# Order of VectorE's work behind a norm: the rest of a chunk behind the first product of the next pair

## The reference, cut to what matters

```python
def _rms_norm(x, w):
    xf = x.astype(jnp.float32)
    y = xf * lax.rsqrt(jnp.mean(xf * xf, axis=-1, keepdims=True) + RMS_EPS)
    return (y * w.astype(jnp.float32)).astype(x.dtype)
...
x = x + _rms_norm(mix, W['norm_mix_post'][i])
h = _rms_norm(x, W['norm_ffn_pre'][i])
...                                   # f = a dense SwiGLU in layer 0, a top-2-of-8 mixture in layer 1
x = x + _rms_norm(f, W['norm_ffn_post'][i])
gate = jax.nn.sigmoid(_rms_norm(x, W['norm_ple'][i]) @ W['ple_w_gate'][i])
x = x + gate * (p[i].astype(x.dtype) @ W['ple_w_proj'][i])
```

## Time and profile before

| | us |
|---|---|
| median of 3 runs | 1734.22 (1734.21 to 1734.29) |
| the profiled execution | 1737.75 |
| its span, first to last instruction | 1736.0 |
| PE busy in the span | 1674.9 (96%) |
| VectorE busy | 690.6 (40%) |
| ScalarE busy | 568.2 (33%) |
| GpSimd busy | 254.1 (15%) |
| mean granted clock of TensorE | 0.98 |

### The profile page before, as it was taken

How to read it: one execution, slowest core, us unless ns; L and a number is a source line. 1 busy time by engine, 2 the same in 40 slices (tenths; PEclk the granted TensorE clock), 3 DMA queues, 4 the chain that set the end, 5 groups by cost and what they waited for, 6 DMA issues and landing times.

```text
span 1736.0 us, 29438 instructions
## 1 busy us (share of the span) xinstructions
PE 1674.9 (96%) x12422; PEld 1542.4 (89%) x12422; DVE 690.6 (40%) x1039; ACT 568.2 (33%) x955; POOL 254.1 (15%) x323
## 2 busy tenths in 40 slices
PE   7999998999999998989999979999999999999988
PEld 6877898999999997988778968998988989889988
DVE  3444355444244434554444552314133142242355
ACT  5232444322122323442324452313233132231252
POOL 5643121000000001206421012000000000002010
PEclk9999999999999999999999986999999999999999
DMA  5345261323232321313352325787877877879312
GB/s 171 87 87 114 75 208 60 92 90 113 71 97 85 115 80 49 127 56 80 89 114 73 103 104 195 234 284 243 276 281 227 290 258 245 295 233 340 114 50 86
DMA packets 73062, 260.02 MB, mean 150 GB/s; under 512 B 10152, under 2 KB 10672, under 8 KB 72928
## 3 DMA queue, kind: packets, MB, share of 16 engines
q1 hardware_dynamic: 59760, 219.52, 38.9%
q0 software_dynamic: 13184, 38.79, 8.0%
HBM read 237.20 MB, written 21.31 MB: 149 GB/s over the span
## 4 chain that ended last, share of the span: by engine, by line
PE 92%; DVE 3%; ACT 2%; issue 1%; DMA 1%; ACTq 0%; DVEq 0%; SPq 0%; POOL 0%; POOLq 0%
PE lin L728 72%; PE aux L728 18%; DVE h_lo L1784 1%; DVE zreg L1781 1%; DMA region_y<-yslot,idxg 1%; ACT h_hi L1266 1%; PE aux L1031 1%; DVE zreg L1784 0%; DVE x L1781 0%; PE aux L1033 0%; DMA wreg<-in_w_in_slabs 0%; ACT region_y L1266 0%; PE aux L873 0%; PE aux L875 0%; ACT zreg L1297 0%
## 5 line engine op out<-in xcount | busy, mean ns | idle before, releaser
L728 PE MATMUL lin<-h_hi,whi 128*128 128x260 f32 x1616 | 434.1, 289 | 23.2 <-DVE h_lo L1784 23.2
L728 PE MATMUL lin<-h_lo,whi 128*128 128x260 f32 x1616 | 425.9, 285 | 0.0
L728 PEld LDWEIGHTS lin<-h_hi,whi 128*128 128x128 f32 x1616 | 309.3, 191 | 32.9 <-issue 27.3
L728 PE MATMUL lin<-h_hi,wlo 128*128 128x260 f32 x1616 | 329.1, 286 | 0.0
L728 PEld LDWEIGHTS lin<-h_lo,whi 128*128 128x128 f32 x1616 | 309.0, 191 | 0.6
L728 PE MATMUL lin<-zreg,wreg 128*128 128x160 f32 x2048 | 284.2, 301 | 1.7 <-issue 1.7
L728 PEld LDWEIGHTS lin<-zreg,wreg 128*128 128x128 f32 x2048 | 280.6, 191 | 4.8 <-issue 4.7
L728 PEld LDWEIGHTS lin<-h_hi,wlo 128*128 128x128 f32 x1616 | 252.8, 191 | 0.0
L1781 DVE TENSOR_TENSOR wlo<-wreg,whi 128x1024 fp32r<-128x1024 f32 (+1 forms) x140 | 180.5, 1290 | 90.1 <-ACT whi L1266 90.1
L1266 ACT ACTIVATE whi<-wreg 128x1024 fp32r<-128x1024 f32 (+1 forms) x140 | 152.0, 1089 | 68.2 <-DMA wreg<-in_ffn_w_down 26.9
L1781 DVE TENSOR_TENSOR region_b<-zreg,lin 128x160 f32<-128x160 f32 x88 | 28.2, 321 | 320.8 <-PE lin L728 320.8
(11 more groups left out here) (341 smaller groups left out, 2454.8 us busy)
## 6 DMA issues: line engine op xcount, KB each, us to landing
wreg<-in_moe_w_gate SPq DMA_DIRECT2D x64, 512.0 KB, 5.2
wreg<-in_moe_w_up SPq DMA_DIRECT2D x64, 512.0 KB, 6.0
wreg<-in_moe_w_down SPq DMA_DIRECT2D x56, 512.0 KB, 4.5
wreg<-in_w_in_slabs SPq DMA_DIRECT2D x44, 512.0 KB, 3.6
ring_more<-in_moe_w_gate SPq DMA_DIRECT2D x24, 512.0 KB, 4.6
ring_more<-in_moe_w_up SPq DMA_DIRECT2D x24, 512.0 KB, 4.5
wreg<-in_ffn_w_gate SPq DMA_DIRECT2D x22, 512.0 KB, 3.5
wreg<-in_ffn_w_up SPq DMA_DIRECT2D x22, 512.0 KB, 3.4
```

The lines of the kernel that those rows point to most:

```text
L728: return nc.tensor.matmul(out, lhsT, rhs, start=start, stop=stop)
```

## The change

```diff
             def normed(N, w, h=None, sums=None):
 
-                for c in range(DC + 2):
-                    if h is not None and c >= 2:
+                def product(c):
+                    if N or c >= 2:
+                        dve.wait_ge((x_dve, x_pool)[c % 2], N * DC // 2 + c // 2)
+                    stt(ut[:, c % 2], acc[:, c], cols[:, w + c:w + c + 1], rn, ALU.mult, ALU.mult).then_inc(ut_ready, 1)
+                for c in range(0, DC + 2, 2):
+                    if c < DC:
+                        product(c)
+                    if h is not None and c:
                         low_h(*h, c - 2)
                     if c < DC:
-                        if N or c >= 2:
-                            dve.wait_ge((x_dve, x_pool)[c % 2], N * DC // 2 + c // 2)
-                        stt(ut[:, c % 2], acc[:, c], cols[:, w + c:w + c + 1], rn, ALU.mult, ALU.mult).then_inc(ut_ready, 1)
-                    if c % 2 and c < DC:
-                        dve.wait_ge(ut_ready, N * DC + c)
-                        tt(x[:, c - 1], x[:, c - 1], ut[:, 0], ALU.add).then_inc(x_dve, 1)
+                        product(c + 1)
+                        dve.wait_ge(ut_ready, N * DC + c + 1)
+                        tt(x[:, c], x[:, c], ut[:, 0], ALU.add).then_inc(x_dve, 1)
+                    if h is not None and c:
+                        low_h(*h, c - 1)
                     if sums is not None:
                         add_squares(sums, c - 2)
+                        add_squares(sums, c - 1)
```

## The result

The changed kernel takes 1740.63 us (median of twenty executions, 1735.80 to 1742.56); the kernel before, timed beside it, 1737.66 (twenty, 1731.95 to 1740.74; the three shown ahead of the prediction are among them, at 1734.21 to 1734.29). The ratio is 1.0019, with a 95% interval of 1.0012 to 1.0026: **slower by 3.3 us, between 2.1 and 4.5** (the ratio is not that of the two medians, which lie 3.0 us apart). The profiled execution took 1740.95 with a span of 1739.2.

A forecast was written before the change was run, and what follows sets the result against it. PE was taken to bound the kernel (92% of the span), VectorE's order mattering only where PE waits. Stage terms 0.84 + 0.81 - 0.06 + 0.65 = +2.2 us on 1734.22 gave 1736.4, range 1734.3 to 1739.2.

The forecast's parts named there:

- stage 3's term: Sums of stage 3: three held as before, only others; PE's last sum gains 0.06 us, bounds 0 and -0.5.
- The holds: VectorE instructions with two SBUF inputs, issued while GpSimd adds, wait for that addition and end 0.55 to 0.56 us later.
- The base: Level for the whole kernel: the earlier runs' median of 1734.22 us, to which +2.2 was added, giving 1736.4.
- The size of the effect: Whole kernel: a measurement tells about 0.2% (3.5 us) from no change; slower by more 19%, faster by more 6%.
- clock case: Stage 2: PE's longer waits lower the clock for one or two turns; +3.6 to +5.0 us in all; 18%.
- No hold: Moved products and rests run free beside GpSimd's additions in the stages; 4.1 us faster, 1730.1; 5%.
- absorbed: R1 gets the port ahead of GpSimd, or later waits swallow the shifts; 1734.3 to 1735.5 us; 14%.
- Two signs: R1, R3 and R5 at some 1.7 to 1.8 us; a new PE wait before chunk 1 in stages 1 and 2.
- Stage 1: R0 ends 0.67 us later, chunk 1 starts at 281.17 instead of 280.33: +0.84, bounds 0.67 and 1.5.
- Stage 2: R1 comes 2.2 us later, 1.4 returns as the wait for R6 vanishes: +0.81, bounds -0.2 and 3.8.
- Stage 4: PE's last wait is for R5 instead of R6, then 5.58 us of work: +0.65, bounds 0.2 and 1.2.

The follow-up runs named there:

- again: The changed kernel unaltered, profiled a second time in one execution: 1735.75 us.
- after5: The changed kernel unaltered, timed again in twelve executions: 1740.29 us, ratio to the kernel before 1.0014.
- stage2_old: The changed kernel with the old order in stage 2 alone: 1740.86 us, ratio to the kernel before 1.0018.
- filled: The changed kernel with 18 idle matmuls on PE before chunk 1 of stage 2: 1741.61 us, ratio to the kernel before 1.0033.
- filled3: The changed kernel with six idle matmuls on PE before chunk 1 of stage 2: 1738.15 us, ratio to the kernel before 1.0014.
- stage2_new: The kernel before with the new order in stage 2 alone: 1738.33 us, ratio to the kernel before 1.0005.
- all_vector: The changed kernel with GpSimd's four additions of each norm moved to VectorE: 1733.30 us, ratio to the kernel before 0.9993.
- the best order tried: All additions on VectorE, in stages 1 and 2 each early one right behind its product, otherwise the changed order: 1731.28 us, ratio to before 0.9958.

## Why the prediction was wrong, and where it was right

Four steps failed. The sum was put on the wrong level: that is 3.4 us, and without it the time lies in the range. A change of +2.2 us was called no change. The fall of the clock in stage 2, 1.4 us in its stage, was given 18% and left out of the sum. And stage 3's term was −0.06 where +0.38 was measured. The holds and the other terms stand.

**The base.** 1736.4 was 4.2 us too low, and 3.4 of that is the level: I added the change to the three executions' 1734.22, while twenty give 1737.66. The profiled execution, 1737.75, stood 3.5 above the three, and I set that aside. Three values within 0.1 us of each other looked like a level; executions of this kernel run from 1731 to 1742. Set on 1737.66, the same +2.2 would have given 1739.9 and a range of 1737.7 to 1742.6, with 1740.63 in it.

**The size of the effect.** I forecast +2.2 and called it a change within 0.2%, that is, none. With twenty executions a side the interval is 0.07% to either side, so +2.2 us (0.13%) is itself a slower kernel that can be told from no change. The mechanism pointed to slower with 80% (forecast and clock case); I turned this into 19% by too wide a bound on the measurement.

**The holds**: right, and they carry nearly all the rest. P2 at 1.67 to 1.69 in stages 1, 2 and 4, R1, R3 and R5 at 1.79 to 1.81 in stages 1 and 4, P2 ending where R0 had ended, R0 0.67 later (4.45 after P0 instead of 3.77 in stage 2). "No hold" (5%) and "absorbed" (14%) did not come about: no rest got ahead of GpSimd in any profile, though a sum did once. Two signs were set too wide: in stage 2 only R1 is held (1.77), while R3 and R5 take 0.76, and PE's wait in front of chunk 1 there was not new but grew from 0.43 to 1.92. The sum for stage 2 used R1 alone and is not touched by that.

**Stage 1**: the mechanism right, the size in part. PE's first wait 6.12, forecast 6.1; chunk 1 at 281.29, forecast 281.17, with P0 0.11 later than in the trace of before. At the stage's end +0.42, under the forecast's lower bound of 0.67, and +0.55 to +0.82 in the other profiles with the new order there and the same lost clock (`again`, `after5`, `stage2_old`, `filled`, `filled3`). In the first profile the clock rose a little earlier against the matmuls: PE worked 4.58 us at the lower level there (5.51 before), and 5.3 to 5.4 in those with +0.75 or more.

**Stage 2**: the mechanism right, the clock case weighed too low. I gave 18% to a fall of the clock, priced at 1.4 for one turn. It came in all five profiles with R1 behind the addition there and no filler, at 1.0 to 2.1 in its stage over the 31.81 of `filled3` (1.4 in the first). The row I leaned on was 0.92 idle in four us at clock 1.00, against a stop of 3.66 with a fall; the new place, 1.42 and 1.92 with six matmuls between, I took, with 18%, to be nearer to the first. It is nearer to the second. Another step is doubtful: I let the 1.4 run through to the end of the program. In the half kernels it did not: `stage2_old` was no quicker without the low clock, and `stage2_new` had it at a mean clock no lower than that of the kernel before. For the whole change the plain losses, 2.4 and 3.3 us, can't tell 2.2 from 3.6. Without the clock the stage loses 0.79 (`filled3`), forecast 0.81.

**Stage 3**: wrong, +0.38 instead of −0.06. I stepped VectorE by 0.67 everywhere. Two sums behind each other step by 0.81, held or not (2.59 for two and 3.40 for three after; 2.30 for three in `all_vector`), where two additions to different chunks step by 0.61 (1.30 for two). In `add_squares` each sum waits on `sq_used` for the one before it (L1817) and adds to its result; that this is the reason was not tested. Three such steps are 0.42 of the 0.44 that the forecast missed. In the order before, products stood between the sums and hid most of that; the row was there, 2.58 for S5 and S6, of which 1.78 is the hold and 0.80 the step.

**Stage 4**: right. +0.68, forecast 0.65; last wait for R5, 5.57 to the next slab, forecast 5.58.

Without the clock in stage 2 the stages give some 0.8 + 0.8 + 0.4 + 0.7 = 2.7, the forecast's terms with stage 3 put right. At equal clock the time shows 2.0 (1.4 to 2.7). That the forecast's +2.2 comes so near to this 2.0 is partly luck, with stage 3's term 0.4 off.

## What to carry to other kernels

Work put into an engine's gap is free only if the gap is that engine's own: here VectorE's wait lay exactly beside GpSimd's addition. P2, moved into it, was held, the odd rests moved behind VectorE's addition were held by the next one on GpSimd, and the rests for which PE waits came later. Before you move work around such a neighbour, ask what it costs to do without it: with four additions a stage back on VectorE, the changed order went from 2.0 us over the kernel before to 4.1 under it at equal clock, and the best order tried to 5.2 under it; no order around GpSimd that was tried beat the kernel before. And where the scatter is as large as the effect, fix the level with as many executions as the comparison will have, and look at time against mean clock before a stage's loss is put down as the program's.

## What was not expected of the hardware

- A gap need not be unbroken to take the clock down: after waits of 1.42 and 1.92 us with six matmuls between them, the granted clock was 0.83, 0.50 and 0.82 in the next three stretches of 2 us, though PE was busy for 1.4 to 2.0 us of each; with 1.48 us of filler in the second wait it stayed at 1.00.
- The loss comes in equal pieces. Of the places where profiles lose clock, most lose 1.7 us of full clock or twice that (stage 1: 1.7, 3.4 or 5.1 in different kernels' profiles, and 22.8, 24.0 to 25.0 or 26.1 us). The largest loss is another, in every profile: 17 to 19 us in one stretch behind stage 3, from 1034 on in the kernel before.
- Which places lose a piece changes from one execution to the next, also where PE is busy throughout and the code is the same: of the changed kernel's three profiles one has low clock at 918 and 1573, the two others at 862 and at 865.
- An instruction that starts during another engine's can still go first: once in 156 cases S5 did, and GpSimd's addition took 2.29 us instead of 1.66 to 1.71.
